# A two-layer block on one core: the conditioning vectors made stationary in four column groups, and the recurrent branch moved three gate products later

## The reference, cut to what matters

```
def _modulate(x, cond, norm_g, w_ada, b_ada):
    mod = jax.nn.silu(cond) @ w_ada + b_ada        # (1024) @ (1024 x 3072), for two vectors
    shift, scale, gate = jnp.split(mod[:, None, :], 3, axis=-1)
    return rmsnorm(x, norm_g) * (1.0 + scale) + shift, gate
```

```
u = conv_b + sum(xp[:, j:j + s] * conv_w[j] for j in range(C_CONV))
r = sigmoid(blockwise(u) @ wa + ba);  i = sigmoid(blockwise(u) @ wx + bx)
a = exp(-LRU_C * r * softplus(-lam));  h = scan(a, sqrt(1 - a*a) * i * u)
y_c = h * gelu(yc)
gates = sigmoid(gt + b_gate)                        # 3 x 1024 columns: the gate products
```

## Time and profile before

| | us |
|---|---|
| three runs | 3954.23, 3945.95, 3941.73 (median 3945.95) |
| profiled execution, first to last instruction (span) | 3950.5 |
| TensorE busy | 3589.2 (91%) |
| VectorE busy | 1908.9 (48%) |
| ScalarE busy | 1348.4 (34%) |
| GpSimd busy | 237.2 (6%) |
| modulation matmuls, TensorE busy | 108.9 in 768 passes |
| mean granted TensorE clock | 0.942 |

### The profile page before, as it was taken

The page is one execution under the profiler, slowest core; times in us unless marked ns, Lnnn a source line. Parts: engine busy times, 40 slices in busy tenths (PEclk is TensorE's granted clock), DMA queues, the critical chain, the costliest instruction groups (busy, mean ns, idle before and its releaser), DMA issues. The chain is left out here.

```text
span 3950.5 us, 44451 instructions
## 1 busy us (share of the span) xinstructions
PE 3589.2 (91%) x18426; PEld 2836.7 (72%) x18426; DVE 1908.9 (48%) x3579; ACT 1348.4 (34%) x2445; POOL 237.2 (6%) x342
## 2 busy tenths in 40 slices
PE   7999989997989999999999988888798998888888
PEld 5888867664777888888766577777686665676676
DVE  4599952443834323322566644445345444224443
ACT  3211253544212211111322334444324555324441
POOL 1011110000100000000000000000000000000000
PEclk9699998998999999999999998988798999889999
DMA  3223321000521111111201011000221000000112
GB/s 113 91 100 119 128 107 55 29 22 36 204 96 32 49 51 56 48 43 46 99 29 35 24 34 34 27 29 23 105 74 53 32 32 26 27 24 16 34 50 84
DMA packets 69289, 228.90 MB, mean 58 GB/s; under 512 B 8728, under 2 KB 12824, under 8 KB 69088
## 3 DMA queue, kind: packets, MB, share of 16 engines
q1 hardware_dynamic: 43056, 132.68, 10.2%
q0 software_dynamic: 22576, 80.80, 6.0%
q10 hardware_dynamic: 3456, 12.58, 0.8%
HBM read 179.37 MB, written 36.17 MB: 55 GB/s over the span
## 5 line engine op out<-in xcount | busy, mean ns | idle before, releaser
L2421 PE MATMUL PS<-m,m 128*128 128x512 f32 (+3 forms) x3560 | 1426.3, 402 | 96.0 <-DVE m L2767 18.8
L2423 PE MATMUL PS<-m,m 128*128 128x512 f32 (+3 forms) x3560 | 1368.5, 386 | 0.0
L2422 PE MATMUL PS<-m,m 128*128 128x512 f32 (+3 forms) x3560 | 1366.9, 385 | 0.0
L2421 PEld LDWEIGHTS PS<-m,m 128*128 128x128 f32 (+2 forms) x3560 | 681.1, 192 | 300.1 <-issue 43.6
L2423 PEld LDWEIGHTS PS<-m,m 128*128 128x128 f32 (+2 forms) x3560 | 681.3, 192 | 135.6 <-issue 1.6
L2422 PEld LDWEIGHTS PS<-m,m 128*128 128x128 f32 (+2 forms) x3560 | 684.7, 193 | 120.2 <-issue 2.3
L2767 DVE TENSOR_TENSOR m<-m,m 128x1024 fp32r<-128x1024 f32 (+5 forms) x204 | 210.7, 1033 | 423.9 <-ACT m L2609 422.9
L2701 ACT COPY m<-PS 128x512 f32<-128x512 f32 x352 | 205.4, 589 | 458.1 <-PE PS L2528 457.4
L2538 PE MATMUL PS<-m,m 128*64 128x256 f32 (+1 forms) x1408 | 310.4, 413 | 28.4 <-ACT m L2701 21.2
L2519 PE MATMUL PS<-m,m 64*128 64x256 f32 (+5 forms) x1968 | 253.6, 369 | 62.5 <-ACT m L2690 43.5
L2519 PEld LDWEIGHTS PS<-m,m 64*128 64x128 f32 (+1 forms) x1968 | 214.5, 198 | 111.3 <-ACT m L2690 54.3
(11 more groups left out here) (190 smaller groups left out, 3037.1 us busy)
## 6 DMA issues: line engine op xcount, KB each, us to landing
m<-in_w SPq DMA_DIRECT2D x220, 512.0 KB, 3.3
g_scratch<-m ACTq DMA_DIRECT2D x24, 512.0 KB, 2.6
m<-g_scratch POOLq DMA_DIRECT2D x24, 512.0 KB, 4.7
m<-in_w SPq DMA_DIRECT2D x32, 256.0 KB, 2.6
x_scratch<-m POOLq DMA_DIRECT2D x2, 4096.0 KB, 13.5
m<-m POOLq DMA_DIRECT2D x60, 128.0 KB, 2.7
m<-in_xT POOLq DMA_DIRECT2D x24, 256.0 KB, 7.8
y_scratch<-m POOLq DMA_DIRECT2D x12, 512.0 KB, 2.9
```

The lines of the kernel that those rows point to most:

```text
L2421: pe.e.engine.matmul(o, L[0], X[0], start=start, stop=False)
L2422: pe.e.engine.matmul(o, L[0], X[1], start=False, stop=False)
L2423: return pe.e.engine.matmul(o, L[1], X[0], start=False, stop=stop)
```

## The change

- A call of `modulate()` now takes four K slices (one half r of K) of 512 weight columns (block c of 6): four fp32 matmuls, each with two stationary columns (the conditioning vectors) and 512 moving weight columns, which write rows 0-1, 32-33, 64-65 and 96-97 of bank 7. Two calls (r = 0, 1) accumulate one block. There are 24 calls.
- After each second call ACT copies bank 7 to SBUF (`modrows`, 12 times), and at the start of the next call TensorE adds the four row groups and turns them (`modt`: four fp32 matmuls against a 128x2 selection matrix), into bank 6. DVE clears bank 7 once at the start.
- Both ring buffers are used by one call, and loaded again after it.
- Calls now stand: 1 in stage 1, 2 before the index products, 6 among them (after every fourth head), 4 in `cx`/`cy`, 11 in the even gate products 0 to 20.
- `lambda` stands before the index products. `LRU_AT` is 20, 21, 22, 23.

```
-LRU_AT = [17, 18, 20, 21]
+LRU_AT = [20, 21, 22, 23]
...
-    tiles += [(f"{x}{m}", 8, 128) for x in ("ea", "oa") for m in range(24)]
+    tiles += [(f"{x}{m}", 2, 512) for x in ("ea", "oa") for m in range(24)]
...
+    p.add("modclear", d=bank(7))
...
+    def m_turn():
+
+        while m_held:
+            key, rows = m_held.pop()
+            at_ = 3072 + (48 if key[0] == "od" else 0) + 8 * key[1]
+            p.add("modt", key=key, parts=[(PS[:, at_ + 2 * i:at_ + 2 * i + 2], rows[:, 128 * i:128 * i + 128]) for i in range(4)],
+                  pick=cc("pick"))
+            m_free[:] = [(S.modt, key)]
...
-        p.add("mod", of=kind, m=m_, L=[ring[n % RING][:, 128 * k:128 * k + 128] for k in range(8)],
-              o=PS[:, at_:at_ + 2], csil=csil, after=(S.ring[n % RING], ("ea", n)))
+        for i in range(4):
+            k, x = 4 * r + i, (2 * n + i // 2) % RING
+            parts_.append((PS[32 * i:32 * i + 2, 3584:4096], csil[:, 2 * k:2 * k + 2], ring[x][:, 512 * (i % 2):512 * (i % 2) + 512]))
+        p.add("mod", key=m_all[n], parts=parts_, first=r == 0, free=bank_free[7] if r == 0 else [],
+              after=[(S.ring[(2 * n + i) % RING], ("ea", 2 * n + i)) for i in range(2)])
+        if r:
+            p.add("modrows", key=(kind, c), done=(S.mod, m_all[n]), d=m_rows[:, :], o=bank(7), free=list(m_free) + list(rows_free))
...
-            for _ in range(3):
-                steps_of(ik, 2)
-                modulate()
+            steps_of(ik, 6)
+            modulate()
...
-                    if nr % 3 == 0:
-                        modulate(nr > 18)
+                    if nr % 4 == 0:
+                        modulate(nr == 24, [(S.lru, "lambda")])
...
-                    if n == 7:
+                    if n == 7 and n_g % 2 == 0 and m_next[0] < len(m_all):
                         modulate()
...
-            for k in range(8):
-                m = e.matmul(s["o"], s["L"][k], s["csil"][:, 2 * k:2 * k + 2], start=k == 0, stop=k == 7)
-            m.then_inc(*pe.says(S.mod, (s["of"], s["m"])))
+            for o, L, X in s["parts"]:
+                m = e.matmul(o, L, X, start=s["first"], stop=not s["first"])
+            m.then_inc(*pe.says(S.mod, s["key"]))
+        elif s.kind == "modt":
+            pe.wait_ge(S.evac, ("mod",) + s["key"])
+            for o, L in s["parts"]:
+                m = e.matmul(o, L, s["pick"], start=True, stop=True)
```

More of the change, by code:

```diff
@@ L1229, in schedule @@
         ring = [mem([P, T]) for _ in range(RING)]
-    m_bank = {"ev": 6, "od": 7}
-    m_all = [(kind, m_) for kind in ("ev", "od") for m_ in range(24)]
-    m_next, m_fetched = [0], [0]
+        m_rows = mem([P, 512])
+        assert mem.at <= low_end - 3 * 4 * T
+    m_all = [(kind, c, r) for kind in ("ev", "od") for c in range(6) for r in range(2)]
+    m_next, m_fetched, m_held, m_free = [0], [0], [], []
+    p.add("modclear", d=bank(7))
     def m_fetch(upto, after=()):
@@ L1236, in m_fetch, with modulate @@
             n = m_fetched[0]
[L1237 to L1238 removed]
+            kind, c, r = m_all[n // 2]
+            at_ = W_AT[f"{kind[0]}a{4 * c + 2 * r + n % 2}"][0]
             p.add("eload", n=n, out=ring[n % RING][:, :], in_=w[at_:at_ + P * 1024].rearrange("(p c) -> p c", p=P),
[L1240 removed]
+                  signal=S.ring[n % RING], free=list(after) + [(S.mod, m_all[(n - RING) // 2])] * (n >= RING))
             m_fetched[0] += 1
[L1243 removed]
+    def m_turn():
[5 more added lines that the diff above has]
+            m_free[:] = [(S.modt, key)]
+    def modulate(last=False, rows_free=()):
         n = m_next[0]
         m_next[0] += 1
[L1247 to L1250 removed]
+        m_turn()
+        kind, c, r = m_all[n]
+        parts_ = []
+        for i in range(4):
[5 more added lines that the diff above has]
+            p.add("modrows", key=(kind, c), done=(S.mod, m_all[n]), d=m_rows[:, :], o=bank(7), free=list(m_free) + list(rows_free))
+            bank_free[7] = [(S.evac, ("mod", kind, c))]
+            m_held.append(((kind, c), m_rows))
         if not last:
[L1252 removed]
+            m_fetch(2 * (n + 1) + RING)
     def first_norm(c, sums=None):
@@ L1386, in schedule @@
             modulate()
+            p.add("lambda", blam=[blam[:, 64 * i:64 * i + 64] for i in range(4)], ld=ld[:, :], lam=lam_t, after=t_blam,
+                  sink=vc("sink", 0, 8), nsink=nsink[:, :])
             k_t = end("k", 0) + end("k", 1)
@@ L1395, in schedule @@
             end("q1", 1)
-            modulate(last=True)
-            ring = late_ring
-            m_fetch(m_next[0] + RING, normed + [(S.mod, m_all[m_next[0] - 1])])
+            ring, m_rows = late_ring, late_rows
+            m_fetch(2 * m_next[0] + RING, normed + [(S.mod, m_all[m_next[0] - 1])])
             b = take()
@@ L1448, in schedule @@
             ring = [mem([P, T]) for _ in range(RING)]
-            m_fetch(m_next[0] + RING, [(S.mod, m_all[m_next[0] - 1])])
+            m_rows = mem([P, 512])
+            assert m_rows is not late_rows and mem.at == rows_at + 2048
+            m_fetch(2 * m_next[0] + RING, [(S.mod, m_all[m_next[0] - 1])])
             xc_t, gl_t = [], []
@@ L1501, in schedule @@
             st["lo"] = "dve"
-            for kind in ("ev", "od"):
-                b, (mod, gs) = m_bank[kind], mods[kind]
-                o = PS[:, 512 * b:512 * b + 48].rearrange("p (a c) -> p a c", c=2)
+            m_turn()
+            for n, kind in enumerate(("ev", "od")):
+                mod, gs = mods[kind]
+                o = PS[:, 3072 + 48 * n:3072 + 48 * n + 48].rearrange("p (a c) -> p a c", c=2)
                 bb = vc(f"{kind}_b", 0, 24).rearrange("p (a c) -> p a c", c=1).to_broadcast([P, 24, 2])
@@ L2495, in tensor_program @@
             pe.wait_ge(S.gateact, "cond")
-            pe.wait_ge(*s["after"])
-            for k in range(8):
-                m = e.matmul(s["o"], s["L"][k], s["csil"][:, 2 * k:2 * k + 2], start=k == 0, stop=k == 7)
-            m.then_inc(*pe.says(S.mod, (s["of"], s["m"])))
+            pe.wait_ge(S.clear, "mod")
+            for ev in s["after"]:
+                pe.wait_ge(*ev)
+            for ev in s["free"]:
+                pe.wait_ge(*ev)
+            for o, L, X in s["parts"]:
[5 more added lines that the diff above has]
+                m = e.matmul(o, L, s["pick"], start=True, stop=True)
+            m.then_inc(*pe.says(S.modt, s["key"]))
         elif s.kind == "lrugate":
@@ L2660, in scalar_program @@
             e.activation(s["relu"], s["ps"], ACT.Relu).then_inc(*act.says(S.evac, n))
+        elif s.kind == "modrows":
+            act.wait_ge(*s["done"])
+            for ev in s["free"]:
+                act.wait_ge(*ev)
+            e.copy(s["d"], s["o"]).then_inc(*act.says(S.evac, ("mod",) + s["key"]))
         elif s.kind == "cond":
@@ L2764, in vector_program @@
                 dve.wait_ge(*ev)
+        elif s.kind == "modclear":
+            e.memset(s["d"], 0.0).then_inc(*dve.says(S.clear, "mod"))
         elif s.kind == "wprep" and s["on"] == "dve":
```

25 lines of the change are left out of this document (12 added, 13 removed).

## The result

The changed kernel takes 3895.85 us (median of four runs, 3893.72 to 3902.45) against 3946.4 us of the kernel before in the same comparison (four runs, 3941.73 to 3954.23): a ratio of 0.9872 with a 95% interval of 0.9858 to 0.9886, so 50 us faster. The forecast was 3892 us.

A forecast was written before the change was run, and what follows sets the result against it. TensorE, busy 91% of the span, was taken as the bound, DVE's top-k and conv second. Stage terms -10.5 - 3.7 - 10.9 - 28.7 = -53.8 us, from the median 3945.95, gave 3892 us, own range 3878 to 3904.

The forecast's parts named there:

- The call: New modulation call on TensorE: four column groups stream at once, 1.15 us a call, about 2.2 at the low clock.
- stage 4: `cx` to the end of `ak0`, 459.5 us before: forecast 430.8 us, a change of -28.7, bounds -22 and -34.
- Stage 1: Start of the kernel up to L2457, with one call in place of three: -10.5 us.
- Stage 2: Up to the first index product: TensorE waits for the key copy, `lambda` delays it about 2.8 us; -3.7 us.
- copies slowed further by loads: The smaller-gain bound before the first index product: loads slow the key copies, leaving only -1 us.
- Stage 3: Index products, 54.9 us before: six calls and three turns, forecast 44 us, so -10.9, bounds -7 and -21.
- The feared wait for the ring: Index products: each call needs both ring buffers and two loads take 4.5 us; waits in most calls would show the forecast wrong.
- T: Time mark in the recurrent tail: start of the first L2505, the first recurrent gates; later steps are counted from it.
- Rival 3: Recurrent tail: four consecutive groups make each period 3 to 4 us longer, 15 us more, 3907 us; chance 0.08.
- Behind `ak0`: The rest of the kernel after `ak0`: nothing changes there.
- Rival 4: Index stage and kernel start stay at 1.2 GHz: 6.5 us less gained, 3898 us; chance within the forecast's 0.67.
- rivals 1 and 2: Calls: only pairs of column groups overlap, 2.0 us each, 3917 us, chance 0.16; or none, 3.67 us, 3968 us, 0.06.

The follow-up runs named there:

- e1: Changed kernel with the recurrent groups back behind gate products 17, 18, 20 and 21, so the new modulation calls alone: 3926.91 us, ratio 0.9952 to the kernel before.
- e2: Kernel before with only the recurrent groups moved behind gate products 20 to 23, so the placement alone: 3950.87 us, ratio 1.0001 to the kernel before.
- e5: Changed kernel with the four matmuls of a call in one column group, writing the same two rows: 3950.82 us, ratio 1.0005 to the kernel before.
- e6: Changed kernel with the four matmuls of a call in two column groups, two matmuls each: 3909.61 us, ratio 0.9901 to the kernel before.
- e4: Changed kernel with `lambda` behind the split of `q1` instead of ahead of the key split: 3890.62 us, ratio 0.9855 to the kernel before.

## Why the prediction came out

The forecast of 3892 us was 4 us off, inside its own range, and its two main claims hold: both halves had to be counted together (e1, e2), and the groups run at once (e5, e6). Step by step:

- **The call.** 1.15 us was taken and 0.97 measured (cold 2.2 and 1.82). The form was right, two slots of 0.43; the 0.15 for a change of shape was not there. Over 15 calls of stage 4 that is 2.7 us.
- **Stage 1, -10.5.** The first traces of the two kernels say -11.0, and so would have passed for a hit. Half of it was luck of the clock in the one trace of before: against the second trace and e2's the gain is 5.2 and 5.5 us. The step that failed is taking a single trace's clock in the first 50 us as the kernel's. The changed kernel's two traces have 15.8 us there, both.
- **Stage 2, -3.7.** Nothing was gained. Lambda's delay was seen (2.8 us taken; 2.7 by e4), but the copies are issued 8.5 us behind `q1`'s last matmul where it was 4.8, 3.7 us later, and the landing was priced at 6.2 us where it takes 7 to 8 with the loads of the second call beside it. The bound "copies slowed further by loads" was the case.
- **Stage 3, -10.9.** Measured -15.9. The term that was mis-sized is what the low clock costs. In the first trace the six calls take 8.2 us where six at 2.2 had been counted, since a call at the low clock takes 1.82 and the last ones take 0.97; the three turns 3.8 where 5.25 stood; the heads 25.0 where they took 29.8. The index products ran at 0.55 or 0.56 in every trace of the old calls and between 0.64 and 0.85 in those with four-group calls. Why the clock is higher was not tried apart. The feared wait for the ring was small: 0.8 us in the first trace, 1.3 in the second, 3.9 in e1.
- **Stage 4, -28.7.** Measured -32.8 to the end of `ak0` (426.7 us; forecast 430.8). To the first gates 339.3 us were needed, where 343.7 had been added up: 29 x 10.97 + 15 x 0.97 + 7 x 0.88 = 338.8, so the cold start of 2 us was not there and the calls were 0.2 us cheaper; DVE's conv stood ready 8.3 us ahead of TensorE, some 12 forecast. Behind T the chain was right to 0.7 us: product 22 at T + 22.05 (22.1 forecast, with a wait of 4.08 where 4.3 was taken), product 23 at T + 39.5 (39.6), `aq0` at T + 57.7 (57.1), `ak0` at T + 74.65 (74.4). The waits were forecast for full-speed products. Product 22 took 13.4 us with a start at the low clock, and so the wait ahead of product 23 is 0.23 us and not some 3. Rival 3 (a longer tail) is out.
- **Behind `ak0`.** "Nothing changes" holds for the work, though not for one pair of traces; what differs there is scatter of up to 8 us between two traces.

The errors had both signs, and cancelled: against the means of two traces each, stages 1 and 2 were taken 6 us too good, 3 and 4 nine too bad, so that the sum to the end of `ak0` (-53.8) was 3 us too small; behind it the scatter took 3 us back. That the number came so near is in part luck. The medians differ by 50.6, the spans of the traces by 54.6; the 4 us between the two are of the size by which single executions of a kernel differ. Rival 4 (the change does not reach the clock) is out by the 0.70 and 0.66 of the index stage, rivals 1 and 2 by e5 and e6.

## What to carry to other kernels

Before a saving on the busiest engine is counted, find the engine that is second and how far behind it stands: here 27 of the microseconds saved turned into a wait without the later placement, which by itself is worth nothing. Let fp32 matmuls with a narrow stationary operand write different 32-row groups of a bank: four of them took 0.97 us here, two slots of 0.43, and one alone needs two slots as well (an estimate from the one-group call). And a wait that names an engine tells what came last, not what would be gained: moving the stores that stood in the way lengthened the chain, moving the weight split out of their queue gave 13 us.

## What the runs showed of the hardware that was not expected

- The issue order within an fp32 call: the first passes of all four matmuls start 6 to 7 ns apart, then the second passes 0.43 us later (the starts of the changed kernel's call at 231.53 us).
- A DVE scan of 128 x 1024 took 4.31 us instead of 2.29 when a GpSimd subtraction had started 0.3 us before it.
- Two SBUF to SBUF copies of 256 KB landed in 3.3 us (median) when no load was issued within 2.5 us behind them, in 5.8 to 6.2 in the traces of the old calls, and in 6.9 to 8.1 when two loads of 512 KB were issued within a us of them.
- In stage 1 the profile's clock column says 1.00 while 512-column passes stand 0.427 us apart, almost twice the later 0.227. Here the spacing of the passes shows the clock at the start, and the column does not.
- The moment at which the clock rises in the first 60 us, by the spacing of the passes, was about 47.4 us in the first trace of before and 34.3 in the second, 35.0 in e2. What caused it was not settled.
